# Linear heads: the state product moves next to the weighing, the sums of squares move directly ahead of the next head's scores, and the third-bank scores run first

## The reference, cut to what matters

```python
s = jnp.einsum('bhld,bhsd->bhls', qc, kc) * w_intra
num = jnp.einsum('bhls,bhsv->bhlv', s, vc) + w_inter[..., None] * jnp.einsum('bhlk,bhkv->bhlv', qc, c)
den = jnp.sum(s, axis=-1) + w_inter * jnp.einsum('bhlk,bhk->bhl', qc, n)
h_out = num / jnp.maximum(jnp.abs(den), jnp.exp(-m_t))[..., None]
...
c_new = decay[..., None, None] * c + jnp.einsum('bhs,bhsk,bhsv->bhkv', w_end, kc, vc)
...
h_ml = h_ml * lax.rsqrt(jnp.mean(h_ml * h_ml, axis=-1, keepdims=True) + RMS_EPS)
```

## Time and profile before

| what | value |
|---|---|
| three runs | 2212.98 to 2215.41 us, median 2214.39 us |
| the profiled execution, its own time | 2213.32 us |
| its span in the trace | 2211.5 us |
| TensorE matmul busy | 2199.0 us, 99% |
| VectorE busy | 1548.1 us, 70% |
| ScalarE busy | 947.2 us, 43% |
| GpSimd busy | 276.1 us, 12% |

### The profile page before, as it was taken

One profiled execution on the slowest core, in us unless ns is written; L12 is line 12 of the kernel. 1 busy time (PEld: TensorE's weight loads), 2 busy tenths in 40 slices (PEclk: granted clock), 3 DMA queues, 4 the chain that ended last, 5 costly groups with the idle time before them and its releaser, 6 DMA issues.

```text
span 2211.5 us, 38510 instructions
## 1 busy us (share of the span) xinstructions
PE 2199.0 (99%) x16106; PEld 2155.1 (97%) x16106; DVE 1548.1 (70%) x1796; ACT 947.2 (43%) x1280; POOL 276.1 (12%) x395
## 2 busy tenths in 40 slices
PE   9999999999999999999999999999999999999998
PEld 7999999999999999999999999999988999999998
DVE  7876868657666666667666666666587678768676
ACT  5343444434444443444444444434465434224443
POOL 0000000000200013322421121111000112100000
PEclk9999999999999999999999999999999999999999
DMA  6444353534453545454545455454766767653548
GB/s 182 116 129 112 109 141 106 143 110 124 112 136 109 145 119 150 117 141 115 126 119 139 128 132 134 115 130 109 243 205 183 261 214 226 190 154 86 138 129 268
DMA packets 432843, 323.27 MB, mean 146 GB/s; under 512 B 14477, under 2 KB 394261, under 8 KB 431264
## 3 DMA queue, kind: packets, MB, share of 16 engines
q1 hardware_dynamic: 407808, 254.06, 41.4%
q0 software_dynamic: 24784, 66.24, 10.1%
q10 hardware_dynamic: 80, 0.52, 0.1%
HBM read 257.41 MB, written 63.35 MB: 145 GB/s over the span
## 4 chain that ended last, share of the span: by engine, by line
PE 97%; DVE 1%; DMA 1%; ACT 0%; issue 0%; POOL 0%; SPq 0%; DVEq 0%; POOLq 0%; ACTq 0%
PE pp L1047 67%; PE pp L1273 13%; PE pp L1432 7%; PE M L1065 1%; PE pp L1057 1%; PE M L1361 1%; PE M L1374 1%; PE pp L1529 1%; PE M L1234 1%; PE M L1057 1%; PE M L1319 1%; PE M L1408 1%; PE M L1292 1%; PE pp L1515 0%; PE M L1047 0%; DMA raw_a<-in_w_out_dram 0%
## 5 line engine op out<-in xcount | busy, mean ns | idle before, releaser
L1047 PE MATMUL pp<-xa,wa_hi 128*128 128x288 f32 x7392 | 1480.3, 296 | 0.1
L1047 PEld LDWEIGHTS pp<-xa,wa_hi 128*128 128x128 f32 x7392 | 1185.3, 188 | 1.1 <-DVE zs L2173 0.4
L1047 PE MATMUL pp<-xa,wa_lo 128*128 128x288 f32 x3696 | 1086.7, 294 | 0.0
L1047 PEld LDWEIGHTS pp<-xa,wa_lo 128*128 128x128 f32 x3696 | 696.1, 188 | 0.0
L2061 DVE TENSOR_TENSOR wa_lo<-raw_a,wa_hi 128x1024 fp32r<-128x1024 f32 x262 | 319.2, 1221 | 211.4 <-ACT wa_hi L1551 211.1
L1551 ACT ACTIVATE wa_hi<-raw_a 128x1024 fp32r<-128x1024 f32 x262 | 276.6, 1057 | 204.5 <-PE pp L1047 203.5
L2061 DVE TENSOR_TENSOR wa_lo<-raw_r,wa_hi 128x1024 fp32r<-128x1024 f32 x134 | 177.2, 1323 | 148.9 <-ACT wa_hi L1551 148.9
L1551 ACT ACTIVATE wa_hi<-raw_r 128x1024 fp32r<-128x1024 f32 x134 | 141.4, 1055 | 134.0 <-PE pp L1047 126.7
L1273 PE MATMUL pp<-gt_hi,wb_hi 128*128 128x288 f32 x768 | 167.7, 300 | 0.0
L1273 PE MATMUL pp<-gt_lo,wb_hi 128*128 128x288 f32 x768 | 164.4, 296 | 0.0
L1273 PE MATMUL pp<-gt_hi,wb_lo 128*128 128x288 f32 x768 | 164.2, 296 | 0.0
(11 more groups left out here) (366 smaller groups left out, 2600.8 us busy)
## 6 DMA issues: line engine op xcount, KB each, us to landing
raw_a<-in_w_in_dram SPq DMA_DIRECT2D x202, 512.0 KB, 5.1
raw_r<-in_w_in_dram SPq DMA_DIRECT2D x68, 512.0 KB, 5.1
z_scratch<-zs POOLq DMA_DIRECT2D x52, 576.0 KB, 3.3
raw_b<-in_w_branch_dram SPq DMA_DIRECT2D x48, 512.0 KB, 4.9
gz<-z_scratch SPq DMA_DIRECT2D x48, 288.0 KB, 4.1
raw_a<-in_w_out_dram SPq DMA_DIRECT2D x20, 512.0 KB, 6.3
gt_hi<-gated_scratch SPq DMA_DIRECT2D x4, 1152.0 KB, 7.4
gt_lo<-gated_scratch SPq DMA_DIRECT2D x4, 1152.0 KB, 10.0
```

What stands on the lines that cost most here:

```text
L1047: i = nc.tensor.matmul(out, ws[:, slot, k, :], xa[:, o, part, k, :], start=opens and k == 0 and s == 0, stop=k == HK - 1 and s == 2, skip_ ...
```

## The change

The order of TensorE's steps in a head becomes: scores, weighing, state, sums of squares, with the next head's scores right behind the sums of squares (`ML_SLOTS` has no halves there). The halves per head stay 9, 8, 8 and 7. Three halves now stand between the state and the sums of squares (two in the fourth head). The blocks of the scores are reordered: those of columns 1024 to 1343 (the third bank) first, then the others behind a wait for `ssq_read`. The state waits for the copies of the weighing (`num_ready`) where it waited for `ssq_read`; the sums of squares wait for `state_ready`, which the scores waited for. On VectorE `read_state` moves ahead of the read of the sums of squares. No instruction is added or removed; GpSimd's and SP's lists are the same, and ScalarE's code isn't touched.

```diff
@@ -83,9 +83,9 @@
 SB_SLOTS = [[2, 2]] * 3 + [[2, 1]] * 3
 ML_SEGS = ([(16, 0), (17, 0), (16, 1), (17, 1)] + [(h, s) for h in range(H_SB + 2, H_ML - 2) for s in range(2)]
            + [(30, 0), (31, 0), (30, 1), (31, 1)])
-SCORES, WEIGH, SSQ, STATE = range(4)
-
-ML_SLOTS = [[4, 2, 1, 2], [3, 2, 1, 2], [3, 2, 1, 2], [3, 2, 2, 0]]
+SCORES, WEIGH, STATE, SSQ = range(4)
+
+ML_SLOTS = [[4, 2, 3, 0], [3, 2, 3, 0], [3, 2, 3, 0], [3, 2, 2, 0]]
 
 SB_BLOCKS = [(0, 0, 512, 0), (1, 512, 384, 128), (3, 896, 128, 384), (2, 1024, 256, 256),
              ("past", 1280, 64, TP), (4, 1344, 64, TP)]
@@ -1364,12 +1364,12 @@
             def ml_head(i):
                 pe.wait_ge(mk_loaded, 16 * (i + 1))
                 pe.wait_ge(mq_loaded, 16 * (i + 1))
-                if i:
-                    pe.wait_ge(state_ready, i + 1)
-                else:
+                if not i:
                     pe.wait_ge(at_read, SBH)
                     pe.wait_ge(g_ready, PG + SBH)
-                for kb, col, w, q0 in ML_BLOCKS:
+                for kb, col, w, q0 in ML_BLOCKS[3:] + ML_BLOCKS[:3]:
+                    if i and col == 0:
+                        pe.wait_ge(ssq_read, i)
                     for c in range(MC):
                         m = nc.tensor.matmul(M[:, col:col + w], ml_k[:, c, TOKEN0[kb]:TOKEN0[kb] + P],
                                              ml_q[:, c, q0:q0 + w], start=c == 0, stop=c == MC - 1)
@@ -1391,14 +1391,7 @@
                 m.then_inc(num_done, 1)
                 for h, s in ml_segs(i, WEIGH):
                     seg(h, s)
-                for b in range(2):
-                    pe.wait_ge(squares_ready, 2 * i + b + 1)
-                    m = nc.tensor.matmul(M[:, 512 * b:512 * b + TH], ones[:, :], W_ml[:, b * TH:(b + 1) * TH],
-                                         start=True, stop=True)
-                m.then_inc(ssq_done, 1)
-                for h, s in ml_segs(i, SSQ):
-                    seg(h, s)
-                pe.wait_ge(ssq_read, i + 1)
+                pe.wait_ge(num_ready, 3 * (i + 1))
                 pe.wait_ge(kw_ready, i + 1)
                 for c in range(MC):
                     for stream, blocks in enumerate((range(NT), [NT])):
@@ -1409,6 +1402,14 @@
                                                      start=kb == blocks[0] and s == 0, stop=kb == blocks[-1] and s == 2)
                 m.then_inc(state_done, 1)
                 for h, s in ml_segs(i, STATE):
+                    seg(h, s)
+                pe.wait_ge(state_ready, i + 2)
+                for b in range(2):
+                    pe.wait_ge(squares_ready, 2 * i + b + 1)
+                    m = nc.tensor.matmul(M[:, 512 * b:512 * b + TH], ones[:, :], W_ml[:, b * TH:(b + 1) * TH],
+                                         start=True, stop=True)
+                m.then_inc(ssq_done, 1)
+                for h, s in ml_segs(i, SSQ):
                     seg(h, s)
 
             for i in range(MLH):
@@ -2637,7 +2638,7 @@
                     decay_rows(0)
                 else:
                     gated_lo(PG + SBH + MC * (i - 1), zml[:, 0, :])
-                    merges(i - 1, STATE)
+                    merges(i - 1, SSQ)
                 split_lo(At(h + 2))
                 dve.wait_ge(scores_done, i + 1)
                 dve.wait_ge(Wm_ready, i + 1)
@@ -2682,26 +2683,25 @@
                 nc.vector.scalar_tensor_tensor(den[:, :], den[:, :], DEN_MIN, EM_h[:, :], ALU.max, ALU.max).then_inc(dmax_ready, 1)
                 split_lo(At(h + 5))
                 merges(i, WEIGH)
+                read_state(i)
+                merges(i, STATE)
                 dve.wait_ge(ssq_done, i + 1)
                 dve.wait_ge(norm_act, norm_step(i, 3))
                 nc.vector.scalar_tensor_tensor(two(den[:, :]), M[:, 0:1024].rearrange("p (b t) -> p b t", b=2)[:, :, 0:TH],
                                                1.0 / MDH, two(den[:, :]), ALU.mult, ALU.add).then_inc(ssq_read, 1)
                 dve.wait_ge(norm_act, norm_step(i, 4))
                 steps.link(nc.vector.reciprocal(den[:, :], den[:, :]))
-                merges(i, SSQ)
                 if i < MLH - 1:
-                    read_state(i)
                     decay_rows(i + 1)
                 gate(i)
                 if i == MLH - 1:
                     for c in range(MC):
                         gated_lo_direct(PG + SBH + MC * i + c, ML_STORED + c, zml[:, c, :])
-                    read_state(i)
                 steps.end(1)
 
             for i in range(MLH):
                 ml_head(i)
-            merges(MLH - 1, STATE)
+            merges(MLH - 1, SSQ)
 
             def out_lo(m, src):
                 dve.wait_ge(wa_hi_ready, made(m))
```

## The result

| | median | runs |
|---|---|---|
| before | 2214.07 us | 2212.98 to 2215.41 us, 4 |
| changed | 2243.76 us | 2242.25 to 2243.94 us, 4 |

The ratio is 1.0133, with a 95% interval of 1.0121 to 1.0145: 29.7 us slower. The forecast was 2225.7 us (2220 to 2233), slower. The direction held; the time lies 10.8 us above the range.

A forecast was written before the change was run, and what follows sets the result against it. TensorE, almost always busy, was taken to bound the kernel. Waits of 10.3 us at three weighings plus 1.6 in the fourth head, 11.9 on top of 2213.3, gave 2225.2, put at 2225.7 us (2220 to 2233).

The forecast's parts named there:

- What bounds the kernel: TensorE has matmuls in flight 2199.0 of 2211.5 us; no instruction is removed, so added waits on it make it slower.
- State moved forward, third-bank scores first: On TensorE in each head: neither the earlier state nor the reordered scores waits; both put at nothing.
- The fourth head: In seg(32, 1): TensorE waits 1.6 us for VectorE's low part; the gated loads land in time, covered by 0.9 us.
- Rival 3: Something else late: load for seg(32, 1) 1 to 3 us past cover, or projection weights; 2227 to 2230 us; chance 0.09.
- The chain: From sums of squares to mv_lo: weighing may start at 18.77 us, TensorE arrives at 15.33; three waits of 3.4 us.
- rival 1: TensorE's clock falls in the new gaps, costing 0 to 3.5 us a fall; 2231 to 2236 us; chance 0.15.
- the sum of 11.9: Total added TensorE wait in us: 10.3 at three weighings plus 1.6 in the fourth head.

The follow-up runs named there:

- run 3: Changed kernel with GpSimd's n_out stores held until the last gated loads landed, and slots [4,2,1,2] putting two halves between sums and scores: 2215.15 us.
- run 6: As run 5, with VectorE's gate and first low part of the gated result moved behind mv_lo of the next head: 2215.60 us.
- run 1: Changed kernel with GpSimd's two n_out stores held until the last loads of the gated operand have landed: 2235.48 us.
- run 7: Kernel before the change, with three quarters of the two n_out stores issued as seg(31, 1) ends, just ahead of the last gated loads: 2221.75 us.
- run 2: Changed kernel with slots [4,2,1,2]: one half behind the state, two between the sums of squares and the scores: 2223.66 us.
- run 8: Changed kernel with late n_out stores, VectorE waiting for GpSimd's mask ahead of its gate, so idle while the mask runs: 2241.90 us, one execution.
- run 5: Changed kernel with late n_out stores, and the next head's exponents ahead of the reciprocal on VectorE: 2226.09 us.

## Why the prediction was wrong

The waits came where the prediction put them. Three terms of its sum were wrong: the granted clock in the gaps, put at nothing (6.2 us at the weighings and 1.8 behind the transfer); the load for `seg(32, 1)`, put at nothing with 0.9 us to spare (6.1 us more than VectorE's 1.6); and GpSimd's mask, taken at its old length (3.0 us over three heads).

**What bounds the kernel; no gain to be had.** Right. Runs 3 and 6 keep the new order of the steps, run 6 also the scores directly behind the sums; both lose the gaps, and neither is faster than before.

**State moved forward, third-bank scores first: nothing.** Right for TensorE: no wait at the state, at the sums or in the scores. The sentence on GpSimd in that part is one of the steps that failed. It says that the two state stores start earlier and that only finished things stand ahead of them in the queue; I did not ask what stands behind them. The two `n_out` stores do. Before, they left at 1915.77, after the gated loads had landed; after the change

```profile
1925.44 0.90 POOL L3140 DMA_DIRECT2D out_dram<-n_out  x1
1926.33 0.88 POOL L3141 DMA_DIRECT2D out_dram<-n_out  x1
```

(timeline of GpSimd, changed kernel), and the loads left at 1927.64 and 1928.04, behind them:

```profile
gt_hi<-gated_scratch SPq DMA_DIRECT2D x1, 576.0 KB, 13.1
gt_lo<-gated_scratch SPq DMA_DIRECT2D x1, 576.0 KB, 14.6
...
out_dram<-n_out POOLq DMA_DIRECT2D x2, 4.0 KB, 11.5
```

**The fourth head: 1.6 us and "a thin cover".** The VectorE part was right (1.7 in runs 1 and 3); with the loads at 14.6 us in place of 5.9 the wait was 7.7, and 1.8 more with the clock. Rival 3 had named this load, at 1 to 3 us past its cover, and 9 in 100. Measured: 9.5 us where the sum had 1.6. Runs 1 and 7 show the cause from both sides.

**The chain: 18.77 us, 3.4 a gap.** The mechanism, the place and the number of gaps were right; the size was 19.77 and 4.4. The first term that was off is the mask. I took 3.43 us from the earlier trace rows and found VectorE's own queue later by 0.2, so that a longer mask would show in full above that. In its new place the mask ran beside the gate, a low part and a split, and took 4.47. The multiplication, forecast at 12.85, came at 13.76. VectorE's own queue was mis-sized as well: the split beside the mask took 1.75 us where it took 1.22 and ended 13.5 us after the sums started, only 0.3 ahead of the multiplication. Runs 2, 6 and 8 show that the mask's length hangs on what VectorE does beside it: 3.48 us with the merges back ahead of the split, 1.84 in the reciprocal, 1.85 beside nothing. The cost is 1.0 us a head, 3 in all.
The Trainium skill ("SBUF — State Buffer", "SBUF: two separate sides") says that GpSimd and a VectorE operation with two SBUF inputs take turns at one port pair, each holding it for the whole instruction. The runs agree: beside the reciprocal, which has one input, the mask took 1.84 us, beside two-input operations up to 4.47, and with a merge that reads PSUM in the place of the split 3.43. The split that ran beside the mask was longer too, 1.75 us and not 1.22. That the gaps repeat and don't grow was right.

**The clock (rival 1, 0.15).** This was the truth, not a rival: three falls at the weighings cost 6.2 us, a fourth at the transfer 1.8. What I weighed wrongly is the one fall at the program's end. I read "4.1 us after the engine went idle" as if it were a threshold, and 3.4 as under it. In the changed kernel the fall came about 3 us into the first gap, and in run 5 it came after a gap of 2.5 us. The price, 0 to 3.5 us a fall with 1.7 as the middle, was good: 2.7, 1.8, 1.7 and 1.8, the first three with 0.2 us each that isn't the clock's.
The Trainium skill ("TensorE: Matmul & The Clock Gate", "HAM oscillation — how this bites in real kernels") had it that gaps between bursts make the clock fall again and again; the trace agrees at all four gaps of the changed kernel, and run 5 at one gap in three. The case deserved more than 0.15.

In terms of the sum of 11.9: 3.0 more for the mask, 6.2 and 1.8 for the clock, 6.1 for the transfer: 29.0, against 28.9 to the last matmul. The mask or the transfer alone would have stayed inside the range, the clock alone would have reached its end (2225.7 + 8.0 = 2233.7); together, and with the later landing of the last stores, they went 10.8 us past it.

What stays open: when the clock falls in a gap of 2.5 us and when not, which of the two `n_out` stores holds back the load, and why the last output stores landed later in some executions.

## What to carry to other kernels

Where TensorE is 99% busy, an order is judged by the spare time of what hides behind it: lay the other engines' queue out from the step that is moved, and compare with TensorE's own work to the next wait. When a step of a queue moves forward, follow what is queued behind it as well, above all stores of single 4-byte elements that may now leave ahead of loads which someone needs. A wait of 2.5 to 4.5 us on a busy TensorE can cost more than itself, since the clock may fall too: 1.5 to 2.5 us a fall here, against a weighing at the full clock behind a wait.

## What the runs showed of the hardware

GpSimd's mask (four multiplications over 576 columns in all, both operands in SBUF) took 1.84 to 1.85 us with VectorE idle or in the reciprocal (runs 8 and 6), 3.43 beside gate, low part and merge (before), and 4.47 beside gate, low part and split (changed kernel). Two stores of 3 KB in 4-byte elements, one issued 0.6 us ahead of a 576 KB load on another queue and one 0.3 us behind it, made that load land after 13.9 us and not 5.9 (run 7); with two stores of 4 KB, both ahead, it took 14.6 (changed kernel). And TensorE's granted clock went to 1.2 GHz at a moment when the engine had been back at work for more than 1 us after a 2.5 us gap (run 5).
